# A fused encoder block: one projection as seven block products, its weight sums made during attention

## The chip, the cores and the metric

The kernel runs on one core of a Trainium2 chip. The metric is the device time of one execution in microseconds. The core's engines work side by side, each through its own list of instructions: TensorE (PE in the profile; PEld is its loading of weights), VectorE (DVE), ScalarE (ACT), GpSimd (POOL) and SyncE (SP), which here only issues DMAs. They wait for each other through semaphores.

## The reference

One layer of an encoder, in float32, for 512 + 256 tokens with 16 meta tokens; width 1024, MLP width 4096.

```python
u = _rms(h, norm_mix[l])
proj = u @ w_in[l]
...
attn = _mla_attention(q_n, q_r, k_n, k_r, v).reshape(B, L, N_HEADS * V_DIM) @ w_o_attn[l]
a, b = jnp.split(conv_in, 2, axis=-1)
c = a * jax.nn.sigmoid(b)
c = lax.conv_general_dilated(...) + conv_b[l]
c = jax.nn.silu(_layernorm(c, conv_ln_g[l], conv_ln_b[l]))
conv = c @ w_conv_out[l]
g_a, g_c = jnp.split(jax.nn.sigmoid(gate_logits + b_gate[l]), 2, axis=-1)
h = h + (g_a * attn + g_c * conv) @ w_out[l]
u = _rms(h, norm_mlp[l])
h = h + jnp.square(jax.nn.relu(u @ w_mlp_in[l])) @ w_mlp_out[l]
```

The final RMSNorm follows. The change concerns `c @ w_conv_out` and the sums of weight blocks that this product, `w_out` and `w_mlp_out` use.

## The kernel before, in words

**Products.** Every float32 product is three matmuls of rounded parts: of each operand a *high* is made (a copy in the rounded type, on ScalarE) and a *low* (the operand minus its high, on GpSimd or VectorE), and high x high, high x low and low x high are added in PSUM. The 768 tokens are the columns, as 512 + 256, or as two halves of 384 (THIRD).

**Seven block products.** The output projection (units U_OUT), the first MLP product (U_IN) and the second (U_FF) are done as seven products of 2 x 2 blocks in place of eight: each product takes one block or a signed sum of blocks of either side. Sums of weight blocks are needed for them: `isums`, `osums` and `wsums` in DRAM, each made by a DMA copy of one block (issued by SP) and an accumulating DMA of the next one (issued by GpSimd, `accum_op=ALU.add`); those of the MLP are made during the stages before, those of the second MLP in attention, four sums, two halves per pair of heads (lines 730 and 1907). Three-block sums and negated blocks of the MLP are made in the ring itself: ScalarE negates a landed block (line 1159) and GpSimd adds the second block to it by DMA (line 2015).

**The stages around the change.** Attention runs over four pairs of heads. Then comes the attention branch's projection (U_O, 8 units of 128 output rows), its result gated into `zacc` by VectorE (line 1581); beside it the convolution branch's LayerNorm is finished: squares on ScalarE (1089), their sum on GpSimd, the variance by a matmul with ones after unit 4, root (1097), reciprocal (1604), scaling (1591), silu (1102), highs (1105) and lows (1596) of c. Then the convolution branch's projection (U_CO, 8 units, matmuls of line 543): per unit m VectorE multiplies the result in PSUM with the gate (`gconv`, 1646) and adds it to `zacc` (1651). Between these it makes the sums (`zsum`, 1622) and lows (`zlo`, 1629) of zacc's blocks that the output projection reads, and ScalarE their highs (1120). The output projection (matmuls of line 2343) and the MLP (2373 and 2394) follow.

**Order.** There is no scheduler: each engine's list is written out by hand, and an engine runs it in that order. The weights come through a ring of raw slots loaded by SP, each load waiting until a slot's last user is done; high slots are fewer than raw ones, so ScalarE's highs follow TensorE's units closely.

## Time and profile before

| | us |
|---|---|
| median of 3 runs (lowest, highest) | 1244.06 (1241.23, 1245.78) |
| the profiled execution | 1243.28 |
| its span in the trace | 1241.7 |
| TensorE busy | 1211.0 |
| VectorE busy | 895.5 |
| ScalarE busy | 553.6 |
| GpSimd busy | 431.2 |

The profile is of one execution. Busy time is the time in which an engine worked at instructions; span is first to last instruction. The chain of waits goes back from the last instruction to what released each step. The mean granted clock of TensorE is 0.999 of 2.4 GHz. Attention fills the stretch to 577 us, the attention branch's projection that to 637, the convolution branch's that to 705, the output projection that to some 763, and the two MLP products the rest.

### The profile page before, as it was taken

To read this page: it belongs to the slowest core of one execution; us is meant where nothing else is said; L and a number is where in the kernel's file an instruction comes from. 1 tells how busy PE (TensorE), PEld (TensorE's weight loads), DVE (VectorE), ACT (ScalarE), POOL (GpSimd) and SP (SyncE) were. 2 spreads that over 40 slices of the span, in tenths; PEclk is the share of its full clock that TensorE was granted. 3 is DMA by queue.
4 is the path that set the end of the run, shared out by engine and by line. 5 is a ranking of instruction groups with operands and counts; after the bars stand their busy time and mean duration, and the time that the engine had idled before them with its cause. 6 is when DMAs were issued, how large, how long until landed. Compare 5 with 4: busy or idle time off the path is not lost.

```text
span 1241.7 us, 18362 instructions
## 1 busy us (share of the span) xinstructions
PE 1211.0 (98%) x6797; PEld 1075.9 (87%) x6797; DVE 895.5 (72%) x1043; ACT 553.6 (45%) x814; POOL 431.2 (35%) x299
## 2 busy tenths in 40 slices
PE   6999999999999999999999999999999999999997
PEld 5888888888888889987888888999989988887886
DVE  4115999999986666677374766586769796677887
ACT  6234211222245666664352346545553244445555
POOL 2454434488855555464744263000120000002101
PEclk9999999999999999999999999999999999999999
DMA  6347888899899796957798343334793343348633
GB/s 194 94 136 158 201 200 177 203 232 236 190 252 230 168 226 177 274 109 182 201 215 247 107 135 119 109 130 122 181 204 120 120 152 127 128 134 207 176 129 118
DMA packets 174370, 211.70 MB, mean 170 GB/s; under 512 B 13040, under 2 KB 125742, under 8 KB 174301
## 3 DMA queue, kind: packets, MB, share of 16 engines
q1 hardware_dynamic: 136300, 155.19, 40.3%
q0 software_dynamic: 35696, 49.29, 24.3%
q10 hardware_dynamic: 2304, 6.29, 1.3%
q8 instruction: 45, 0.74, 0.2%
q14 instruction: 25, 0.20, 0.0%
HBM read 201.31 MB, written 88.08 MB: 233 GB/s over the span
## 4 chain that ended last, share of the span: by engine, by line
PE 79%; issue 6%; DMA 5%; POOL 3%; DVE 3%; ACT 3%; SPq 1%; POOLq 0%; ACTq 0%; DVEq 0%
PE psum L543 34%; PE psum L2394 17%; PE psum L2373 14%; PE psum L2343 5%; DMA raw<-in_w_mlp_in 2%; PE psum L2196 2%; PE psum L2226 1%; POOL wlo L530 1%; PE psum L2069 1%; DMA rawx<-in_w_mlp_in 1%; DMA wsums<-in_w_mlp_out 1%; PE psum L2208 1%; DMA rawx<-in_w_mlp_out 1%; POOL isums L1902 0%; DVE olo L1536 0%
## 5 line engine op out<-in xcount | busy, mean ns | idle before, releaser
L530 POOL TENSOR_TENSOR wlo<-raw,whi 128x1024 fp32r<-128x1024 f32 (+1 forms) x72 | 167.9, 2332 | 200.0 <-ACT whi L525 199.8
L1377 DVE SCALAR_TENSOR_TENSOR psum<-cs,convw,psum 128x799 f32<-128x799 f32 x196 | 189.4, 1049 | 0.0
L543 PE MATMUL psum<-uhi,whi 128*128 128x512 f32 x592 | 152.4, 338 | 0.8 <-POOL wlo L530 0.8
L543 PE MATMUL psum<-uhi,wlo 128*128 128x512 f32 x592 | 152.9, 339 | 0.0
L543 PE MATMUL psum<-ulo,whi 128*128 128x512 f32 x592 | 152.5, 339 | 0.0
L525 ACT ACTIVATE whi<-raw 128x1024 fp32r<-128x1024 f32 (+1 forms) x73 | 72.1, 987 | 108.3 <-PE psum L543 97.5
L543 PEld LDWEIGHTS psum<-uhi,whi 128*128 128x128 f32 x592 | 91.4, 188 | 14.8 <-POOL wlo L530 1.6
L543 PEld LDWEIGHTS psum<-uhi,wlo 128*128 128x128 f32 x592 | 91.6, 188 | 12.9
L2373 PE MATMUL psum<-u2hi,whi 128*128 128x384 f32 x296 | 100.0, 338 | 2.5 <-DVE rawlo L1772 1.4
L543 PEld LDWEIGHTS psum<-ulo,whi 128*128 128x128 f32 x592 | 91.5, 188 | 12.5
L2373 PE MATMUL psum<-u2hi,rawlo 128*128 128x384 f32 x304 | 101.7, 334 | 0.0
L2373 PE MATMUL psum<-u2lo,whi 128*128 128x384 f32 x296 | 99.0, 334 | 0.0
L1168 ACT ACTIVATE whi<-raw 128x1024 fp32r<-128x1024 f32 x55 | 58.1, 1058 | 76.7 <-PE psum L2394 40.7
L2394 PE MATMUL psum<-whi,hidhi 128*128 128x512 f32 x222 | 86.4, 389 | 0.0
L2394 PE MATMUL psum<-whi,hidlo 128*128 128x512 f32 x222 | 86.4, 389 | 0.0
L2394 PE MATMUL psum<-rawlo,hidhi 128*128 128x512 f32 x216 | 84.0, 389 | 0.0
L2015 POOL DMA_DIRECT2D raw<-in_w_mlp_out x6 | 7.2, 1195 | 214.0 <-ACT raw L1159 214.0
L1758 DVE TENSOR_TENSOR hid<-hid,psum 128x768 f32<-128x768 f32 x64 | 59.5, 951 | 30.0 <-ACT hid L1241 19.2
L2373 PEld LDWEIGHTS psum<-u2hi,whi 128*128 128x128 f32 x296 | 55.6, 188 | 3.4 <-DVE rawlo L1772 1.9
L2373 PEld LDWEIGHTS psum<-u2hi,rawlo 128*128 128x128 f32 x304 | 57.1, 188 | 0.0
L935 ACT ACTIVATE gout<-psum,vec 128x768 f32<-128x768 f32 x16 | 14.4, 902 | 93.9 <-PE psum L543 93.9
L2373 PEld LDWEIGHTS psum<-u2lo,whi 128*128 128x128 f32 x296 | 55.6, 188 | 0.0
(294 smaller groups left out, 3099.2 us busy)
## 6 DMA issues: line engine op xcount, KB each, us to landing
raw<-in_w_in SPq DMA_DIRECT2D x38, 512.0 KB, 4.4
isums<-in_w_mlp_in SPq DMA_DIRECT2D x32, 512.0 KB, 7.8
isums<-in_w_mlp_in POOLq DMA_DIRECT2D x32, 512.0 KB, 8.1
wsums<-in_w_mlp_out SPq DMA_DIRECT2D x32, 512.0 KB, 10.5
wsums<-in_w_mlp_out POOLq DMA_DIRECT2D x32, 512.0 KB, 10.1
raw<-isums SPq DMA_DIRECT2D x24, 512.0 KB, 3.3
raw<-wsums SPq DMA_DIRECT2D x20, 512.0 KB, 3.2
raw<-in_w_mlp_out SPq DMA_DIRECT2D x16, 512.0 KB, 3.8
```

Source lines behind the costliest of these rows:

```text
L525: nc.scalar.activation(whi[:, c % 2, 0:w], raw[:, c % 4, 0:w], ACT.Copy).then_inc(hi_ready, 1)
L530: gp.tensor_tensor(out=wlo[:, c % 2, 0:w], in0=raw[:, c % 4, 0:w], in1=whi[:, c % 2, 0:w].bitcast(F32), op=ALU.subtract).then_inc(lo_ready, 1)
L543: mm = nc.tensor.matmul(out[:, o0:o0 + n], a, b[:, k, c0:c0 + n], start=first and step == 0, stop=last and step == 2)
L935: nc.scalar.activation(gout[:, c % 2], psum[:, c % 2, 0:TQ], ACT.Sigmoid, bias=vcol("b_gate", i * 4 + c)).then_inc(gate_ready, 1)
L1168: nc.scalar.activation(mhi[high(U_IN + x)], mraw[place(U_IN + x)], ACT.Copy).then_inc(mhi_ready, 1)
L1377: ins = nc.vector.scalar_tensor_tensor(out=out, in0=src, scalar=w, in1=a, op0=ALU.mult, op1=ALU.add)
L1758: nc.vector.tensor_tensor(out=block_, in0=block_, in1=c_banks(m), op=ALU.add if sign > 0 else ALU.subtract).then_inc(hid_added, 1)
L2069: mm = nc.tensor.matmul(bank[:, 2 * n + seg, 0:w], a[:, k], b[:, k, c0:c0 + w], start=k == 0 and step == 0, stop=k == KD - 1 and step == 2)
L2196: mm = nc.tensor.matmul(psum[:, q % 2, e * HALF:e * HALF + n], a[:, c0:c0 + P], b[:, grp["k0"] + k0:grp["k0"] + k0 + n], start=step == 0, ...
L2343: mm = nc.tensor.matmul(bank[:, OUT_MIX[p]["banks"][tt]], a, b[:, kk, :], start=OUT_MIX[p]["new"] and jj == 0 and kk == 0 and step == 0, s ...
L2373: mm = nc.tensor.matmul(bank[:, 2 * in_pair(m) + e, 0:THIRD], a[:, k, e * P:(e + 1) * P], b, start=k == 0 and step == 0, stop=k == KD // 2 ...
L2394: mm = nc.tensor.matmul(bank[:, FF_BANKS[p % 2][tt]], a, b[:, kk, :], start=jj == 0 and kk == 0 and step == 0, stop=jj == STEPS - 1 and kk ...
```

## The change

The convolution branch's projection becomes seven block products as well, each in two halves J of the output rows: 14 units of 4 k x 2 x 3 matmuls with 384 columns (`CO_MIX`). Its four sums of weight blocks (`csums`, of three, two, two and four blocks, the longer ones built on the shorter ones) are made during attention by SP's copies (line 807) and GpSimd's accumulating DMAs (2117), in the place of the fourth sum of the second MLP. That sum is now made in the ring, by an accumulating DMA on the landed block (`x_added`, 2231). The sums of c's blocks are made by VectorE (`c_mix`, 1782 and 1785), 14 highs by ScalarE (1233) and 14 lows by VectorE (1793). A result that two products share is held: ScalarE copies a pair of banks to `xheld` or `zheld` (`co_hold`, 1250), and VectorE's drain (`co_drain`) adds it to another pair (1813), multiplies by a gate block (1816) and adds it to, or takes it from, zacc (1819). The sum of squares moves from GpSimd to VectorE, and the variance's matmul from after unit 4 to after unit 3 of the attention branch. Nearly all weight lows of both projections are GpSimd's now (VectorE keeps those of the convolution branch's units 1 and 2, and loses three of the output projection's), SP's and GpSimd's loops over the pairs are unrolled, and the output projection's seven additions of weight sums become four.

```diff
+CO_UNITS = 2 * 7
-SUMS = (((0, 1), (1, 1)), ((0, 0), (1, 0)), ((1, 0), (1, 1)), ((0, 0), (0, 1)))
+SUMS = (((0, 1), (1, 1)), ((0, 0), (1, 0)), ((1, 0), (1, 1)))
...
+CO_MIX = (
+    dict(a=((0, 0),), b=(0, 0), banks="X", new=True),
+    dict(a=((0, 1),), b=(1, 0), banks="Y", new=True),
+    dict(a=((1, 0), (1, 1), (0, 0)), banks="X", new=False),
+    dict(a=((1, 0), (1, 1)), banks="Z", new=True),
+    dict(a=((0, 0), (1, 0)), banks="X", new=False),
+    dict(a=((1, 0), (1, 1), (0, 0), (0, 1)), b=(1, 1), banks="Z", new=False),
+    dict(a=((1, 1),), banks="X", new=False),
+)
+CO_BLOCKS = ((0, 0, 1), (1, 1, 4), (0, 1, 5), (1, 0, 6))
+C_MIXED = tuple((p, part) for p in (T1, T2, T4, T3) for part in range(2))
+VECTOR_UNITS = (U_CO + 1, U_CO + 2)
...
+            def co_sum_copy(n):
+                sp.wait_ge(copy_landed[3], (STEPS + n) * 16)
+                if n // 2 in (1, 2):
+                    sp.wait_ge(sums_landed[3], (STEPS + n // 2 * 2) * 16)
+                sp.dma_start(co_sum(n), co_term(n, 0)).then_inc(copy_landed[3], 16)
...
-                    for c in range(4):
+                    for c in range(3):
                         sum_copy(c, i * 2 + h)
+                    co_sum_copy(i * 2 + h)
...
+            def gate_block(n):
+                half, tokens, _ = CO_BLOCKS[n % 4]
+                first = KD + 4 * half + n // 4 * 2
+                sp.wait_ge(merged, KD + n - 1)
+                sp.dma_start(gblock[:, n % 2], gates[first:first + 2, :, tokens * THIRD:(tokens + 1) * THIRD]
...
+            def co_hold(J, p, held):
+                act.wait_ge(unit_used, U_CO + 7 * J + p + 1)
+                if p == 0:
+                    wait(act, gated, 7 * J - 2)
+                if p == 2:
+                    act.wait_ge(gated, 7 * J + 1)
+                if p == 3:
+                    wait(act, gated, 7 * J - 4)
+                nc.scalar.activation(held[:, :, :], pair_banks(co_pair(J, p)), ACT.Copy).then_inc(co_held, 1)
...
+            for p, part in C_HIGHS[4:8]:
+                c_high(p, part)
+            co_hi(0)
+            for p, part in C_HIGHS[8:10]:
+                c_high(p, part)
+            co_hi(1), co_hi(2)
+            for p, part in C_HIGHS[10:]:
+                c_high(p, part)
...
+            for v in range(CO_UNITS):
+                J, p = v // 7, v % 7
+                if p in (0, 2):
+                    co_hold(J, p, xheld)
+                if p == 3:
+                    co_hold(J, p, zheld)
+                if v + 3 < CO_UNITS:
+                    co_hi(v + 3)
+                else:
+                    out_hi(v + 3 - CO_UNITS)
...
+            def co_drain(J, e):
+                half, tokens, p = CO_BLOCKS[e]
+                n, done = 4 * J + e, 7 * J + 2 * e
+                held = (xheld, zheld, xheld, None)[e]
...
+                dve.wait_ge(merged, KD + n)
+                dve.wait_ge(unit_used, U_CO + 7 * J + p + 1)
+                if held is not None:
+                    dve.wait_ge(co_held, 3 * J + (1, 3, 2)[e])
+                    nc.vector.tensor_tensor(out=gconv[:, :, :], in0=pair_banks(co_pair(J, p)), in1=held[:, :, :], op=ALU.add).then_inc(gated, 1)
+                    dve.wait_ge(gated, done + 1)
+                dve.wait_ge(gin_landed[n % 2], 16 * (KD // 2 + n // 2 + 1))
...
+            c_mix(T4, 0), c_mix(T4, 1)
+            gate_attn(6)
+            c_low(T1, 0), c_low(T1, 1)
+            gate_attn(7)
+            ring_lo(U_CO + 1)
+            c_low(T2, 0), c_low(T2, 1)
+            ring_lo(U_CO + 2)
+            c_low(T4, 0), c_low(T4, 1)
+            c_mix(T3, 0), c_mix(T3, 1)
+            for p in (T3, 5):
+                c_low(p, 0), c_low(p, 1)
...
+                if p == 2:
+                    pe.wait_ge(co_held, 3 * J + 1)
...
+                if p == 6:
+                    pe.wait_ge(gated, 7 * J + 3)
...
+                if u == 0:
+                    pe.wait_ge(gated, 12)
...
+            def x_add(x):
+                if x_added(x):
+                    if x_negated(x):
+                        gp.wait_ge(wneg_ready, negated_before(x + 1))
                     else:
+                        gp.wait_ge(m_landed[place(U_IN + x)], landed(U_IN + x))
+                        gp.wait_ge(mhi_ready, x - 2)
                     gp.dma_start(x_place(x), x_block(x, 1), accum_op=ALU.add).then_inc(wsum_landed[x % 3], 16)
```

How the rows of an engine's list stand, before and after, at three places. ScalarE where the convolution branch's projection starts, before: silu (L1102), highs of c, weight highs (L525), and the first high of z.

```order
L1102 ACTIVATE cs<-cs,vec 128x768 [waits ln_scaled]
L1105 ACTIVATE chi<-cs 128x768 [waits c_silu]
L525 ACTIVATE whi<-raw 128x1024 [waits unit_used,raw_landed1]
L1102 ACTIVATE cs<-cs,vec 128x768 [waits ln_scaled]
L1105 ACTIVATE chi<-cs 128x768 [waits c_silu]
L525 ACTIVATE whi<-raw 128x1024 [waits unit_used,raw_landed2]
L525 ACTIVATE whi<-raw 128x1024 [waits unit_used,raw_landed3]
L1120 ACTIVATE zhi_118<-zacc 128x768 [waits merged]
L525 ACTIVATE whi<-raw 128x1024 [waits unit_used,raw_landed0]
```

And after: highs of c and of its sums (L1233), weight highs (L1239), the held copies (L1250).

```order
L1239 ACTIVATE whi<-raw 128x1024 [waits unit_used,raw_landed0]
L1233 ACTIVATE chi_125<-csum_139 128x768 [waits mixed] x2
L1239 ACTIVATE whi<-raw 128x1024 [waits unit_used,raw_landed1]
L1239 ACTIVATE whx<-raw 128x1024 [waits unit_used,raw_landed2]
L1233 ACTIVATE chi_123<-csum_137 128x768 [waits mixed] x2
L1233 ACTIVATE chi_124<-cs 128x768 [waits unit_used,c_silu] x2
L1250 ACTIVATE xheld<-psum 128x768 [waits unit_used]
L1239 ACTIVATE whi<-raw 128x1024 [waits unit_used,raw_landed3]
L1239 ACTIVATE whi<-rawx 128x1024 [waits unit_used,m_landed4]
L1250 ACTIVATE xheld<-psum 128x768 [waits gated,unit_used]
L1239 ACTIVATE whx<-rawx 128x1024 [waits unit_used,m_landed5]
```

Four highs of c's blocks, two of them of sums that VectorE makes last, stand directly ahead of the first held copy; before, nothing but weight highs stood there.

VectorE in the convolution branch's projection, before: product with the gate, addition, and between them lows and sums of zacc's blocks.

```order
L1629 TENSOR_TENSOR zlo_124<-zacc,zhi_118 128x768 [waits z_hi]
L1622 TENSOR_TENSOR zsum_135<-zacc 128x768 [waits merged]
L1646 TENSOR_TENSOR gconv<-psum,gin 128x768 [waits merged,gin_landed1,unit_used]
L1651 TENSOR_TENSOR zacc<-zacc,gconv 128x768 [waits merged,gated]
L1646 TENSOR_TENSOR gconv<-psum,gin 128x768 [waits merged,gin_landed0,unit_used]
L1651 TENSOR_TENSOR zacc<-zacc,gconv 128x768 [waits merged,gated]
L1629 TENSOR_TENSOR zlo_124<-zacc,zhi_118 128x768 [waits z_hi]
L1629 TENSOR_TENSOR zlo_129<-zsum_135,zhi_123 128x768 [waits z_hi]
L1622 TENSOR_TENSOR zsum_135<-zacc 128x768 [waits merged]
L1646 TENSOR_TENSOR gconv<-psum,gin 128x768 [waits merged,gin_landed1,unit_used]
L1651 TENSOR_TENSOR zacc<-zacc,gconv 128x768 [waits merged,gated]
```

After, between the drains of the second half's first two blocks (drains 4 and 5):

```order
L1813 TENSOR_TENSOR gconv<-psum,xheld 128x768 [waits co_held,unit_used,merged]
L1816 TENSOR_TENSOR gconv<-gconv,gblock 128x768 [waits gin_landed0,gated]
L1819 TENSOR_TENSOR zacc<-zacc,gconv 128x2x384 [waits gated]
L1865 TENSOR_TENSOR zsum_155<-zsum_154,zacc 128x768 [waits mixed,unit_used,merged]
L1865 TENSOR_TENSOR zsum_157<-zacc 128x768 [waits unit_used,merged]
L1872 TENSOR_TENSOR zlo_148<-zsum_154,zhi_142 128x768 [waits mixed,z_hi]
L1872 TENSOR_TENSOR zlo_146<-zacc,zhi_140 128x768 [waits z_hi]
L1865 TENSOR_TENSOR zsum_156<-zsum_155,zacc 128x768 [waits mixed,unit_used,merged]
L1872 TENSOR_TENSOR zlo_149<-zsum_155,zhi_143 128x768 [waits mixed,z_hi]
L1872 TENSOR_TENSOR zlo_151<-zsum_157,zhi_145 128x768 [waits z_hi]
L1813 TENSOR_TENSOR gconv<-psum,zheld 128x768 [waits co_held,unit_used,merged]
L1816 TENSOR_TENSOR gconv<-gconv,gblock 128x768 [waits gin_landed1,gated]
```

Where one or three instructions stood between two of VectorE's drains, seven now stand between these two, and each drain has three instructions in the place of two.

SP at the end of a pair's loads, before: eight copies for the sums, each waiting only for the copy before it of the same sum.

```order
L730 ISA [waits copy_landed1]
L730 DMA wsums<-in_w_mlp_out 256x1x512
L730 ISA [waits copy_landed2]
L730 DMA wsums<-in_w_mlp_out 256x1x512
L730 ISA [waits copy_landed3]
L730 DMA wsums<-in_w_mlp_out 256x1x512
L730 ISA [waits copy_landed0]
L730 DMA wsums<-in_w_mlp_out 256x1x512
```

After, in the second pair of heads (the loads of the next pair begin at the last row):

```order
L824 DMA wsums<-in_w_mlp_out 256x1x512 [waits copy_landed2]
L807 DMA csums<-csums 128x1024 [waits sums_landed3,copy_landed3]
L824 DMA wsums<-in_w_mlp_out 256x1x512 [waits copy_landed0]
L824 DMA wsums<-in_w_mlp_out 256x1x512 [waits copy_landed1]
L824 DMA wsums<-in_w_mlp_out 256x1x512 [waits copy_landed2]
L807 DMA csums<-csums 128x1024 [waits sums_landed3,copy_landed3]
L846 DMA raw<-in_w_uq 128x4x64 [waits lo_ready]
```

A copy for csums takes the fourth place and waits also for GpSimd's additions to have landed.

## Rows read from the trace of the kernel before

**Rows 1.** The page: TensorE's busy time, and the chain that ended last.
```profile
PE 1211.0 (98%) x6797; PEld 1075.9 (87%) x6797; DVE 895.5 (72%) x1043; ACT 553.6 (45%) x814; POOL 431.2 (35%) x299
...
PE 79%; issue 6%; DMA 5%; POOL 3%; DVE 3%; ACT 3%; SPq 1%; POOLq 0%; ACTq 0%; DVEq 0%
```

**Rows 2.** Windows: start:end, us, each engine's busy us, clock, DMA share, GB/s.
```profile
577.00:637.00 60.00, 60.00 (x334) 51.28 (x334) 36.95 (x29) 27.81 (x31) 37.41 (x20) 1.00 0.90 224
637.00:705.00 68.00, 68.00 (x386) 59.00 (x385) 36.02 (x30) 17.62 (x20) 25.64 (x10) 1.00 0.69 193
```

**Rows 3.** The chain of waits, 577 to 780 us: start, us, what.
```profile
578.34 31.80 PE psum L543 x180
...
611.43 93.28 PE psum L543 x528
704.72 48.97 PE psum L2343 x216
...
771.90 5.23 PE psum L2373 x30
```

**Rows 4.** VectorE in time: start, us, line, names, [idle before <- releaser].
```profile
613.54 4.95 DVE L1604 RECIPROCAL lnr<-lnacc 128x768 f32<-128x768 f32 x1 [2.40 <-ACT lnacc L1097]
...
633.65 1.01 DVE L1591 SCALAR_TENSOR_TENSOR cs<-cs,vec,lnr 128x768 f32<-128x768 f32 x1
...
639.39 0.95 DVE L1581 TENSOR_TENSOR zacc<-psum,gin 128x768 f32<-128x768 f32 x1
...
653.87 0.96 DVE L1646 TENSOR_TENSOR gconv<-psum,gin 128x768 f32<-128x768 f32 x1 [6.53 <-PE psum L543]
```

**Rows 5.** ScalarE in time, in the convolution branch's stage.
```profile
637.64 0.85 ACT L1105 ACTIVATE chi<-cs 128x768 fp32r<-128x768 f32 x1
...
653.93 1.06 ACT L525 ACTIVATE whi<-raw 128x1024 fp32r<-128x1024 f32 x1 [7.42 <-PE psum L543]
```

**Rows 6.** VectorE and GpSimd in time, 629 and 663 us.
```profile
629.48 0.95 DVE L1581 TENSOR_TENSOR zacc<-psum,gin 128x768 f32<-128x768 f32 x1
...
629.63 2.41 POOL L530 TENSOR_TENSOR wlo<-raw,whi 128x1024 fp32r<-128x1024 f32 x1 [4.41 <-ACT whi L525]
...
663.55 3.00 POOL L530 TENSOR_TENSOR wlo<-raw,whi 128x1024 fp32r<-128x1024 f32 x1 [5.47 <-ACT whi L525]
...
664.22 3.15 DVE L1629 TENSOR_TENSOR zlo<-zacc,zhi 128x768 fp32r<-128x768 f32 x1
```

**Rows 7.** The gates' loads, line 780.
```profile
DMA to landing us min/median/max: 2.9/4.7/13.8
```

**Rows 8.** GpSimd's additions in the ring, line 2015, 1100 to 1160 us.
```profile
L2015 POOL DMA_DIRECT2D raw<-in_w_mlp_out x6: 1188/1197/1202, 1119.7 to 1152.4; - x6
...
DMA to landing us min/median/max: 7.2/8.3/9.7
```

**Rows 9.** Waits of TensorE, 1004 to 1242 us: total, times, longest.
```profile
PE psum L2394 <- DVE hidlo L1793: 1.1, 1, 1.1
```

**Rows 10.** The page: DMA issues, KB each, median us to landing.
```profile
wsums<-in_w_mlp_out SPq DMA_DIRECT2D x32, 512.0 KB, 10.5
wsums<-in_w_mlp_out POOLq DMA_DIRECT2D x32, 512.0 KB, 10.1
...
raw<-in_w_mlp_out SPq DMA_DIRECT2D x16, 512.0 KB, 3.8
```

**Rows 11.** SP, GpSimd and ScalarE in time, in attention's second pair.
```profile
393.16 0.39 SPq L752 DMA_DIRECT2D raw<-in_w_uq  x1
...
406.44 1.52 POOL L1907 DMA_DIRECT2D wsums<-in_w_mlp_out  x1
...
436.06 0.63 ACT L525 ACTIVATE whi<-raw 128x512 fp32r<-128x512 f32 x1
```

**Rows 12.** The loads of the next pair's weights, line 752.
```profile
DMA to landing us min/median/max: 2.2/3.9/19.3
```

**Rows 13.** A window of attention, columns as in rows 2.
```profile
416.00:426.00 10.00, 10.00 (x77) 9.59 (x76) 6.81 (x10) 7.38 (x12) 5.09 (x4) 1.00 0.20 53
```

More of the change, by code:

```diff
@@ L234, in x_negated, with x_added @@
     return (IN_MIX[IN_ORDER[x][0]] if x < IN_UNITS else MIX[x // STEPS - len(IN_MIX)]).get("negate", False)
+def x_added(x):
+    return x_negated(x) or (x >= IN_UNITS and len(MIX[x // STEPS - len(IN_MIX)]["b"]) > 1 and
+                            MIX[x // STEPS - len(IN_MIX)]["b"] not in SUMS)
 def negated_before(x):
@@ L242, in summed_before @@
 def summed_before(x, slot):
-    return sum(x_negated(y) for y in range(slot, x, 3))
+    return sum(x_added(y) for y in range(slot, x, 3))
 def posted(p):
@@ new lines, in c_low, with ring_lo @@
+            def c_low(p, part):
+                dve.wait_ge(c_hi, C_HIGHS.index((p, part)) + 1)
+                if p in (T1, T2):
+                    dve.wait_ge(mixed, C_MIXED.index((T2 if p == T1 else T4, part)) + 1)
+                nc.vector.tensor_tensor(out=clo[p][:, 2 * part:2 * part + 2, :], in0=c_source(p, part),
+                                        in1=chi[p][:, 2 * part:2 * part + 2, :].bitcast(F32), op=ALU.subtract).then_inc(c_lo, 1)
+            def ring_lo(n):
+                dve.wait_ge(hi_ready, n + 1)
+                nc.vector.tensor_tensor(out=mlo[place(n)], in0=mraw[place(n)], in1=mhi[high(n)].bitcast(F32),
+                                        op=ALU.subtract).then_inc(inlo_ready, 1)
@@ new lines, in co_drain @@
+            def co_drain(J, e):
+                half, tokens, p = CO_BLOCKS[e]
+                n, done = 4 * J + e, 7 * J + 2 * e
+                held = (xheld, zheld, xheld, None)[e]
+                gate = gblock[:, n % 2]
+                made = zacc[:, 4 * half + 2 * J:4 * half + 2 * J + 2, tokens * THIRD:(tokens + 1) * THIRD]
+                dve.wait_ge(merged, KD + n)
[5 more added lines that the diff above has]
+                dve.wait_ge(gin_landed[n % 2], 16 * (KD // 2 + n // 2 + 1))
+                nc.vector.tensor_tensor(out=gconv[:, :, :], in0=gconv[:, :, :] if held is not None else pair_banks(co_pair(J, p)), in1=gate,
+                                        op=ALU.mult).then_inc(gated, 1)
+                dve.wait_ge(gated, done + (2 if held is not None else 1))
+                nc.vector.tensor_tensor(out=made, in0=made, in1=gconv[:, :, :],
+                                        op=ALU.add if half == 0 else ALU.subtract).then_inc(merged, 1)
@@ L1602, in _ @@
+            gate_attn(0)
+            for j in range(KD):
+                centre(range(j, j + 1))
+                if j > 1:
+                    ln_sq_add(j - 1)
+                if j == 3:
+                    gate_attn(1)
+            ln_sq_add(KD - 1)
+            gate_attn(2), gate_attn(3)
             dve.wait_ge(ln_root, 1)
@@ L2005, in _ @@
-            for u in range(OUT_UNITS):
-                if u not in OUT_VECTOR:
-                    gp.wait_ge(hi_ready, U_OUT + u + 1)
-                    gp.tensor_tensor(out=mlo[place(U_OUT + u)], in0=mraw[place(U_OUT + u)], in1=mhi[high(U_OUT + u)].bitcast(F32),
-                                     op=ALU.subtract).then_inc(lo_ready, 1)
-            def x_add(x):
-                if x_negated(x):
-                    gp.wait_ge(wneg_ready, negated_before(x + 1))
+            out_sum_add(2)
@@ new lines, in _ @@
+            lo_unit(gp, U_O, 0, 4)
+            lo_unit(gp, U_O, 1, 1)
+            out_sum_add(1)
+            lo_unit(gp, U_O, 1, 2)
+            lo_unit(gp, U_O, 1, 3)
+            for n in range(U_CO, U_IN):
+                if n not in VECTOR_UNITS:
+                    gp.wait_ge(hi_ready, n + 1)
+                    gp.tensor_tensor(out=mlo[place(n)], in0=mraw[place(n)], in1=mhi[high(n)].bitcast(F32),
+                                     op=ALU.subtract).then_inc(lo_ready, 1)
+                if n == U_CO:
+                    out_sum_add(3)
@@ L2335, in _ @@
                         h_transposes(n)
-                wh, wl = (w.rearrange("p (k n) -> p k n", k=2) for w in (mhi[high(U_OUT + u)], mlo[place(U_OUT + u)]))
                 for kk in range(2):
```

398 lines of the change are left out of this document (235 added, 163 removed).

## The prediction

> **What bounds the kernel now.** I read the page first, then the table of windows, then the chain of waits, and last the rows in time of each engine around the stages that change. The page says that TensorE is busy 98% of the span and holds 79% of the chain that ended last [rows 1]: time is lost or won where its matmuls become fewer or where it has to wait. The windows show no gap on it from 577 to 705 us, the two branch projections [rows 2]. The chain gives the size of the units there: 93.28 us for 528 matmuls is 11 units of 48, 8.48 us each; the last eight are the convolution branch's, from 636.9 to 704.7 us [rows 3]. VectorE and GpSimd have room in this stage: VectorE works 36 of 68 us and often sits 6.5 us before a unit's gate product, GpSimd works 26 us [rows 2, 4]. This room is what the change spends.
>
> **Matmuls, the gain.** Removed are 8 x 48 matmuls of the convolution branch, 8 x 8.48 = 67.8 us. Added are 14 units of 4 x 2 x 3 = 24 matmuls over 384 columns. The MLP's matmuls of that width take 5.23 us per 30, 0.1743 us each [rows 3], so a unit takes 4.18 us and 336 matmuls 58.6 us: **-9.3 us**. Clock and kind of operand are the same. A rule would make it less: by the Trainium skill, TensorE: Matmul & The Clock Gate, Back-to-back issue gap, a lone matmul costs its columns at 2.4 GHz plus a small fixed term of 2.5 ns. By it a pair of 512 and 256 columns is 325 ns and one of 384 is 162.5 ns, an estimate of 62.4 - 54.6 = 7.8 us won. The rows give 353 ns for the pair and 174 ns for the one, so the measured widths decide.
>
> **The first products and their held banks.** What is new stands ahead of the projection: eight sums of column blocks of c and 14 lows on VectorE, in the place of 8 lows; 14 highs on ScalarE, in the place of 8. In return the variance's matmul goes one unit (8.48 us) earlier, since its sum no longer needs GpSimd; the reciprocal, 4.95 us from 613.54 [rows 4], can start near 605.5 and is over before the gate of unit 4, which ends near 612.4. From there to the end of the last sum (T3) VectorE has 8 scalings, 8 sums, 3 gates and 10 lows, 29 of 0.95 us (six from 633.65 to 639.39 in rows 4), and 2 weight lows of 1024 elements, 1.25 us by their size: 30.0 us, to 642.4. But a VectorE operation with both inputs in SBUF and GpSimd's weight low run one after the other: 0.95 us became 3.15 beside one of GpSimd's, and GpSimd's 2.41 became 3.00 [rows 6]; gates, whose input is PSUM, ran beside one undisturbed [rows 6]. Three weight lows of GpSimd fall in this stretch; with two of them in the way, 2.1 us each, the T3 sums end near 646.6. ScalarE takes its instructions in order, and ahead of the first held copy stand the highs of T3 and of block 5, so three highs of 0.85 us [rows 5] follow the last sum (649.1) and then the copy itself (649.9). Unit 2 needs that copy and its turn is 636.9 + 2 x 4.18 = 645.3: a **wait of 4.6 us**, a new one. Bounds: 0.4 if VectorE never waits for GpSimd, 6.7 with one collision more. I take two, since the one shown and three like it in this stage of before each cost VectorE 2.1 or 2.2 us.
>
> **Drains and the start of the output projection.** In the 58.6 us of the new units VectorE gets 37 operations (22 of the eight drains, 7 sums of z, 8 lows) and GpSimd 12 weight lows. Eight of the 37 read PSUM; the other 29, at 0.95 us, and 12 x 2.41 us on GpSimd [rows 6] exclude each other: 27.6 + 28.9 = 56.5 of 58.6 us. The gaps that VectorE had are gone, and a chain of drains runs behind TensorE. One place in full: unit 13 (its turn 636.9 + 4.6 + 13 x 4.18 = 695.8) waits for the first addition of drain 5. Drain 4 follows the end of unit 8 (679.1) with three operations; then stand seven operations with both inputs in SBUF, and the addition: 679.1 + 11 x 0.95 = 689.6. ScalarE makes the high of S3, for the last of them, only after the held copy that waits for unit 10 (687.5) and a weight high, so the addition ends no earlier than 691. Four weight lows of GpSimd fall in between; three in the way, 2.2 us each, make it 697.7: 1.9 us. In the same way the output projection's unit 0 waits 1.1 us for the last drain's product, unit 2 1.3 us for the sum behind it, and one later unit 1.2 us for its weight low, since all of these lows are GpSimd's now (three were VectorE's) and ScalarE's highs for them stand behind z's highs. Sum **5.5 us**. Bounds: 0 (the operations find the gaps) and 10 (each of the four costs one collision more); gate blocks are loaded behind each drain as before, and gates of the same 0.39 MB landed after 4.7 us in the median but up to 13.8 [rows 7]; at 9 us each drain would start some 4 later.
>
> **One sum of the second MLP in the ring.** The last product of it, 8 units, gets its weight sum by accumulating DMAs from GpSimd in the ring, not from memory. The eight that exist (six of them in the row shown) were issued from 1119.7 to 1152.4, every 4.67 us, against 4.08 us for a unit (18 matmuls of 48.97 / 216 us) [rows 3, 8]; they landed after 8.3 us, and TensorE waited once, 1.1 us [rows 8, 9]. The new ones have no negation ahead of them, and a unit is loaded five units (20.4 us) ahead; load, add, high and low take 3.8 + 8.3 + 1.06 + 1.25 = 14.4 of it [rows 5, 8, 10], and up to six more where the add stands behind the high of the unit two ahead of it. I take **+0.5**; the bounds are 0 and 8 x (4.67 - 4.08) = 4.7.
>
> **Attention.** Eight copies and eight accumulating DMAs of 512 KB go, eight and eight of the same size come. Unrolling the loops of SP and GpSimd changes no order. I take 0 here; the new wait that it hides is a rival. The output projection's weight sums become cheaper (7 additions to 4, on a queue that nobody waited for): 0.
>
> **Sum.** -9.3 + 4.6 + 5.5 + 0.5 = +1.3 us on the profiled execution, whose span of 1241.7 us and 1.6 around it make 1243.3: 1244.6. The median of the runs shown, 1244.06, is 0.8 above that execution, so by it 1245.4; I predict **1245 us**, no difference. What a measurement of this kernel can tell from no change is about 0.5%, 6.2 us.
>
> **Rivals.**
> 1. *Faster: VectorE and GpSimd find their gaps.* If collisions are rarer than I count, the first wait shrinks to 0.4 and the later ones to some 3, the bare order of the drains behind the units: -9.3 + 0.4 + 3 + 0.5 = -5.4, 1238.7 by the median, and with none at all 1234.8. For it: the 6.5 us gaps before each gate product now [rows 4]. Against: every weight low of GpSimd that met an operation of VectorE with two inputs in SBUF cost it time [rows 6]. 0.26; in 0.20 of it the waits are fewer still, and it ends under 1237.8.
> 2. *Slower: SP stands in attention.* SP's copies for the new sums wait for an add of GpSimd to land, and behind them on SP stand the next pair's weight loads. Before, those went out at 393.16 for a high at 436.06 [rows 11]. The add that the copy needs goes out at 406.44 [rows 11] and lands after 10.1 us in the median; the copy then must land before the next one is issued, after 10.5 in the median [rows 10]: the loads go out at 417 + 9 = 426. With the median landing of 3.9 us they are in time; with 13 (the longest was 19.3) [rows 12] they are 3 us late, and so again one pair later. From a landing of 10 us on it decides. Price: 2 x 2.6 = 5.2 us (I take 0.4 of the 3 as slack behind the high), to 1250.6 by the median. For it: landings of over 10 us are common in attention [rows 10]. Against: from 416 to 426 us the DMA share is 0.20 [rows 13], so nothing else stands in their way then. 0.15.
> 3. *Slower by the drains:* gate blocks that land after 9 us, or one more collision at each wait: some 4.3 more, 1249.7. 0.08.
> 4. *The ring cannot keep pace at the end:* +4.7 instead of 0.5, 1249.6. 0.05.
> 5. *It doesn't do what it says:* the matmul count would be as before. The code issues 336 in place of 384; 0.01.
>
> **How the numbers follow.** My forecast (waits that add up to 7 to 13 us in place of 9.3) has 0.45 and its own range is 1241 to 1249. Rivals 1 and 2 put the ends. The range that holds 8 in 10 is **1236 to 1251.5**: below it 0.08, the case with nearly no waits; above it 0.12, rival 2 with a part of 3 or 4. Faster by over 0.5% (below 1237.8): 0.20. Slower by over 0.5% (above 1250.3): 0.20, rival 2 on top of the sum, 3 and 4 with a part of it. Within: 0.60.
>
> **What would show it.** The span of the new units in the chain of waits: 4.18 us a unit and 336 matmuls show the gain. A wait of TensorE's 384-column matmuls for ScalarE's xheld at 645 to 650 us shows the first term; if that wait is absent, the collisions are over-counted. Waits for gconv, zacc and a weight low between 690 and 720 us show the second. Operations of VectorE with 3.15 us beside GpSimd's lows show the mechanism of both. Waits for rawlo or whi of the second MLP's last units show the fourth term; an idle TensorE at 436 to 440 and 487 to 490 us, with SP's copies of csums ahead of the loads, shows rival 2. I am wrong if the fourteen units end more than 4 us away from 636.9 + 58.6 + 4.6 + 1.9 = 702.0, or if attention ends more than 2 us away from where it did.

## The result, and the profile after

| | before | changed |
|---|---|---|
| median of 20 runs, us | 1242.85 | 1247.22 |
| profiled execution, us | 1243.28 | 1249.21 |
| its span, us | 1241.7 | 1247.6 |

The ratio is 1.0031 (95% interval 1.0018 to 1.0043), which is 3.9 us slower; the two medians of the table lie 4.4 us apart. That is inside the band that the prediction called no difference, on the slow side of it, and the interval excludes 1. The changed kernel's trace is of an execution 2.0 us above its median.

First the page of the changed kernel, against [rows 1]:

```profile
PE 1207.2 (97%) x6749; PEld 1078.7 (86%) x6749; DVE 930.3 (75%) x1069; ACT 568.0 (46%) x832; POOL 439.1 (35%) x303
...
PE 79%; DVE 6%; issue 6%; DMA 4%; ACT 2%; POOL 2%; POOLq 0%; SPq 0%; DVEq 0%; ACTq 0%
```

TensorE is busy 3.8 us less and the span is 5.9 us longer; VectorE's share of the chain doubled. Where that is, the windows tell (columns as in rows 2):

```profile
577.00:637.00 60.00, 59.50 (x331) 50.65 (x330) 48.10 (x42) 31.09 (x35) 23.46 (x11) 1.00 0.78 211
637.00:705.00 68.00, 61.85 (x342) 60.80 (x342) 58.59 (x43) 29.87 (x34) 35.59 (x15) 0.95 0.68 211
```

Against [rows 2], TensorE is idle for 6 of 68 us, VectorE works 58.6 us in place of 36.0, and the mean granted clock of the stage is 0.95. The chain of waits at its start (start, us, what) shows both:

```profile
640.64 8.33 PE psum L2555 x48
648.97 4.00 issue
652.97 7.12 PE psum L2555 x26
```

48 matmuls take 8.33 us, 4.17 a unit, as the 384-column row of [rows 3] said. Then comes the wait at unit 2, and the next 26 take 7.12 us where 4.5 would do. Who is waited for, in ScalarE's and VectorE's rows in time, and how TensorE's matmuls follow behind the wait:

```profile
649.00 1.71 ACT L1233 ACTIVATE chi<-csum 128x768 fp32r<-128x768 f32 x2 [6.25 <-DVE csum L1785]
650.62 1.56 ACT L1233 ACTIVATE chi<-cs 128x768 fp32r<-128x768 f32 x2
652.08 0.79 ACT L1250 ACTIVATE xheld<-psum 128x768 f32<-128x768 f32 x1
```

```profile
616.12 9.66 DVE L1760 SCALAR_TENSOR_TENSOR cs<-cs,vec,lnr 128x768 f32<-128x768 f32 x8
...
634.87 4.01 DVE L1782 SCALAR_TENSOR_TENSOR csum<-csum,cs 128x768 f32<-128x768 f32 x2
...
648.02 1.81 DVE L1785 TENSOR_TENSOR csum<-cs 128x768 f32<-128x768 f32 x2
```

```profile
652.97 0.66 PE L2555 MATMUL psum<-chi,whx 128*128 128x384 f32 x1 [4.00 <-issue]
653.43 0.52 PE L2555 MATMUL psum<-clo,whx 128*128 128x384 f32 x1
653.75 0.52 PE L2555 MATMUL psum<-chi,rawlo 128*128 128x384 f32 x1
```

The two rows of 9.66 and 4.01 us are where VectorE met GpSimd's lows (eight scalings and two sums, each row some 2.2 us over its own time). The sums of T3 end at 649.8; four highs stand before xheld, which ends at 652.9. The trace runs 3.8 to 3.9 us later than that of before from the first attention matmul (362.9 against 359.0) to the start of this stage, so in the time of before the wait is where it was forecast. Behind it 15 matmuls come about 0.32 us apart in place of 0.17. In windows:

```profile
649.00:653.00 4.00, 0.03 (x1) 0.06 (x1) 3.96 (x5) 3.97 (x6) 0.00 (x0) 0.79 1.10 349
653.00:660.00 7.00, 7.00 (x27) 7.00 (x28) 6.93 (x4) 1.98 (x3) 5.42 (x2) 0.63 0.06 18
```

The granted clock is 0.63 of 2.4 GHz in the 7 us after 4 us of an idle TensorE: part of them at 1.2 GHz, the rest at 2.4. Set against 0.17 us each, the slow matmuls lose 2.5 us.

The other waits of TensorE, from 637 to 770 us (total, times, longest):

```profile
PE psum L2555 <- issue: 6.2, 2, 4.0
PE psum L2590 <- DVE zacc L1819: 1.2, 1, 1.2
PE psum L2590 <- POOL wlo L2218: 0.8, 1, 0.8
PE psum L2590 <- issue: 0.7, 1, 0.7
```

The two of L2555 are units 2 and 13. These views count only the idle time between two records; measured start to start over the matmul's own time, the five waits lose 4.2, 2.3, 0.8, 1.4 and 1.0 us.

The second of them, at unit 13, is a wait for VectorE's first addition of drain 5 (`gconv`, L1813), and VectorE came to it late. Rows of GpSimd and VectorE in time, between drains 4 and 5:

```profile
690.75 3.07 POOL L2218 TENSOR_TENSOR rawlo<-raw,whi 128x1024 fp32r<-128x1024 f32 x1 [1.75 <-ACT whi L1239]
691.48 3.15 DVE L1872 TENSOR_TENSOR zlo<-zsum,zhi 128x768 fp32r<-128x768 f32 x1
...
694.91 2.86 POOL L2218 TENSOR_TENSOR rawlo<-raw,whi 128x1024 fp32r<-128x1024 f32 x1 [1.09 <-ACT whi L1239]
695.42 3.16 DVE L1865 TENSOR_TENSOR zsum<-zsum,zacc 128x768 f32<-128x768 f32 x1
...
702.45 0.94 DVE L1813 TENSOR_TENSOR gconv<-psum,zheld 128x768 f32<-128x768 f32 x1
702.58 2.37 POOL L2218 TENSOR_TENSOR rawlo<-raw,whi 128x1024 fp32r<-128x1024 f32 x1 [1.74 <-ACT whi L1286]
703.43 2.34 DVE L1816 TENSOR_TENSOR gconv<-gconv,gblock 128x768 f32<-128x768 f32 x1
```

All four weight lows that GpSimd makes between 685 and 701 us hold off an operation of VectorE with two inputs in SBUF, by 2.0 to 2.2 us each. The last weight low that unit 13 itself needs is the one from 694.91; it ended 5.7 us before the unit began, so it was not GpSimd that TensorE waited for.

The stages, each from its first matmul to the next stage's first (the last to the start of its last matmul), in every trace of the study. The first matmul of attention's projection stands among attention's last ones, at 563.6 us in the trace of before; this table begins the stage there.

| trace | attention | attention's projection | convolution's projection | output projection | first MLP | second MLP |
|---|---|---|---|---|---|---|
| before | 204.6 | 73.1 | 67.9 | 58.5 | 241.2 | 229.8 |
| e4, before with unrolled loops | 204.4 | 72.6 | 66.6 | 58.5 | 239.4 | 229.8 |
| changed | 204.5 | 73.1 | 68.1 | 61.3 | 238.8 | 231.3 |
| e10, changed again | 204.4 | 72.7 | 68.4 | 61.3 | 239.1 | 231.2 |
| e1 | 204.5 | 72.4 | 66.9 | 60.6 | 238.2 | 231.8 |
| e2 | 204.4 | 72.4 | 62.7 | 61.7 | 239.4 | 231.5 |
| e3 | 204.6 | 73.1 | 68.0 | 60.6 | 238.6 | 229.7 |
| e5 | 204.3 | 72.5 | 60.1 | 60.7 | 241.4 | 232.9 |
| e6 | 204.5 | 72.7 | 65.6 | 61.4 | 241.1 | 231.5 |
| e7 | 204.6 | 72.4 | 66.3 | 61.3 | 239.9 | 230.8 |
| e8 | 204.5 | 72.4 | 60.1 | 60.7 | 239.2 | 230.2 |
| e9 | 204.4 | 73.1 | 68.0 | 61.3 | 239.4 | 230.0 |

By stages the change costs 0.2 + 2.8 + 1.5 = 4.5 us in the two traces. What lies ahead of attention took 357.3 to 363.0 us over the twelve traces, and the first MLP 238.2 to 241.4. Neither goes with the kernel: e9 is the changed kernel up to the second MLP and has 357.3 where that has 362.9, and the two traces of the same matmuls in before and e4 have 241.2 and 239.4. In e5 and e6 some 1.6 us of the first MLP are again matmuls 0.32 us apart, about ten of them behind a wait of 1.8 us.

### The profile page after: what moved, and what is told of

It is laid out like the page before. It is cut to its first block, busy times and chain, and to the rows that moved or that the text cites. A ratio compares the mean times of both kernels' runs of the same rounds, so it can differ in the third digit from the quotient of the medians.

```text
span 1247.6 us, 18015 instructions
## 1 busy us (share of the span) xinstructions
PE 1207.2 (97%) x6749; PEld 1078.7 (86%) x6749; DVE 930.3 (75%) x1069; ACT 568.0 (46%) x832; POOL 439.1 (35%) x303
## 4 chain that ended last, share of the span: by engine, by line
PE 79%; DVE 6%; issue 6%; DMA 4%; ACT 2%; POOL 2%; POOLq 0%; SPq 0%; DVEq 0%; ACTq 0%
PE psum L584 30%; PE psum L2641 16%; PE psum L2620 15%; PE psum L2555 4%; PE psum L2590 4%; PE psum L2412 3%; PE psum L2442 2%; DMA rawx<-in_w_mlp_in 2%; PE psum L2285 2%; PE psum L2375 1%; DMA raw<-in_w_mlp_in 1%; PE psum L2424 1%; DVE hmix L2003 1%; PE psum L2259 1%; DVE ptlo L1640 1%
## 5 line engine op out<-in xcount | busy, mean ns | idle before, releaser
L571 POOL TENSOR_TENSOR wlo<-raw,whi 128x1024 fp32r<-128x1024 f32 (+1 forms) x64 | 144.7, 2261 | 182.7 <-ACT whi L566 182.5
L2231 POOL DMA_DIRECT2D raw<-in_w_mlp_out x12 | 14.4, 1196 | 258.4 <-ACT raw L1329 209.9
L566 ACT ACTIVATE whi<-raw 128x1024 fp32r<-128x1024 f32 (+1 forms) x64 | 62.5, 977 | 75.7 <-PE psum L584 65.2
L2620 PE MATMUL psum<-u2hi,rawlo 128*128 128x384 f32 x288 | 96.3, 334 | 0.0
L2641 PE MATMUL psum<-whi,hidhi 128*128 128x512 f32 x228 | 89.0, 390 | 1.7 <-DVE hidlo L2014 1.7
L2641 PE MATMUL psum<-rawlo,hidhi 128*128 128x512 f32 x228 | 88.7, 389 | 0.0
L2231 POOL DMA_DIRECT2D raw<-in_w_mlp_in x5 | 6.4, 1288 | 135.8 <-ACT raw L1329 135.8
```

The source lines that it names most:

```text
L566: nc.scalar.activation(whi[:, c % 2, 0:w], raw[:, c % 4, 0:w], ACT.Copy).then_inc(hi_ready, 1)
L571: gp.tensor_tensor(out=wlo[:, c % 2, 0:w], in0=raw[:, c % 4, 0:w], in1=whi[:, c % 2, 0:w].bitcast(F32), op=ALU.subtract).then_inc(lo_ready, 1)
L2620: mm = nc.tensor.matmul(bank[:, 2 * in_pair(m) + e, 0:THIRD], a[:, k, e * P:(e + 1) * P], b, start=k == 0 and step == 0, stop=k == KD // 2 ...
L2641: mm = nc.tensor.matmul(bank[:, FF_BANKS[p % 2][tt]], a, b[:, kk, :], start=jj == 0 and kk == 0 and step == 0, stop=jj == STEPS - 1 and kk ...
```

## The experiments

Each ratio is to the kernel before, timed beside it on the same chip.

**e1.** The first held copy ahead of the last highs.

```diff
             co_hi(1), co_hi(2)
+            co_hold(0, 0, xheld)
+            co_hi(3)
             for p, part in C_HIGHS[10:]:
                 c_high(p, part)
...
-                if p in (0, 2):
+                if p in (0, 2) and v > 0:
                     co_hold(J, p, xheld)
...
-                if v + 3 < CO_UNITS:
+                if v == 0:
+                    pass
+                elif v + 3 < CO_UNITS:
                     co_hi(v + 3)
```

> The first held copy (xheld) and the weight high of unit 3 stand on ScalarE ahead of the highs of T3 and block 5; nothing else is changed. Theory A (ScalarE's order alone makes the 4.0 us wait at unit 2): the wait and the 2.5 us of matmuls at half clock behind it go, and nothing else moves: 6 to 6.5 us less than the changed kernel, 1240.8. Theory B (the order only decides where the wait stands; VectorE and GpSimd, which exclude each other, are the bound of the stage): the wait of unit 2 goes, waits of 1 to 1.4 us appear at units 4 and 5 and the one at unit 13 grows from 2.3 to about 4, the sum of waits stays near 9 to 10 us, and only the clock's 2.5 us are won: 1244.7. If one of the new waits is long enough to lower the clock, even less. I hold B, 0.65.

Measured: 1.0007 (0.9992 to 1.0022). Waits of TensorE, 636 to 775 us:

```profile
PE psum L2559 <- issue: 5.0, 2, 2.8
PE psum L2594 <- POOL wlo L2222: 0.8, 1, 0.8
PE psum L2594 <- DVE zacc L1823: 0.7, 1, 0.7
```

and the windows around the longest:

```profile
655.00:658.60 3.60, 0.79 (x5) 0.50 (x4) 3.53 (x5) 1.06 (x2) 0.00 (x0) 1.00 0.01 3
658.60:662.60 4.00, 4.00 (x15) 4.00 (x16) 3.07 (x2) 3.19 (x4) 2.95 (x2) 0.57 0.48 154
```

The wait at unit 2 is gone and one of 2.8 us stands at unit 4, with a low clock behind it (0.57 over 4 us). Unit 13 waits 2.3 us start to start as in the changed kernel, but here this wait too has a low clock behind it (0.57 from 699.8 to 703.8 us, 1.00 in the changed kernel). The convolution branch's projection has 66.9 us for 68.1: theory A is false. B is right in that the wait moves. It is wrong in where it puts it, in the sum of the waits, which fell from 9.7 to 7.1 us, and in that the clock would be won back: the slow matmuls lose 3.3 us at two places, 2.5 at one in the changed kernel. By the ratios this is 3 us less than the changed kernel, with intervals that overlap; the trace has 1.9 us in the two projections.

**e2.** Weight lows of the convolution branch's units on VectorE. Same order as e1, and eleven `ring_lo` more between VectorE's sums, lows and drains, of which one is shown:

```diff
-VECTOR_UNITS = (U_CO + 1, U_CO + 2)
+VECTOR_UNITS = (U_CO + 1, U_CO + 2, U_CO + 3, U_CO + 4, U_CO + 5, U_CO + 6, U_CO + 7, U_CO + 8, U_CO + 9, U_CO + 10, U_CO + 11, U_CO + 12, U_CO + 13)
...
             co_drain(0, 0)
+            ring_lo(U_CO + 5)
...
```

> As the one before, and VectorE makes the weight lows of all convolution-branch units but the first (11 more, 1.23 us each), GpSimd none of them (it would take 2.41 us each). Theory B (exclusion): time in which either engine holds the other off falls by 11 x 1.2 = 13 us, no operation of VectorE lasts 3.1 us in the stage, the waits in the stage fall from 9.7 us to about 3, and the clock stays up: about 9 us less than the changed kernel, 1238, some 4 to 5 us under the kernel before. Rival (VectorE is full by its own work, 36 us + 13.5 us in 58.6): the lows on VectorE delay the drains, and the time stays at 1245 or above. I hold the first, 0.7.

Measured: 0.9996 (0.9981 to 1.0011). The stage took 62.7 us; this is the first theory, by half of its amount (4.4 us less than the changed kernel, 9 expected). Waits of TensorE in the two projections, 6.4 us start to start where about 3 were expected, and the rows in front of the longest:

```profile
PE psum L2589 <- DVE rawlo L1803: 2.4, 1, 2.4
PE psum L2624 <- DVE zacc L1823: 1.8, 1, 1.8
PE psum L2624 <- POOL wlo L2252: 0.8, 1, 0.8
PE psum L2589 <- issue: 0.8, 1, 0.8
```

```profile
671.53 0.96 DVE L1820 TENSOR_TENSOR gconv<-psum,gblock 128x768 f32<-128x768 f32 x1 [3.73 <-DMA gblock<-gates]
...
673.40 1.22 DVE L1803 TENSOR_TENSOR rawlo<-raw,whx 128x1024 fp32r<-128x1024 f32 x1
```

Until 693 us no VectorE operation of the stage lasts longer than 1.22 us, and VectorE has time to sit idle for a gate block. This block was issued at 662.5, behind 3 MB of h on the same queue, and landed 9 us later; unit 8's low stood behind the drain that needed the block. The remaining 2.4 us of wait did not lower the clock (1.00 in the 4 us behind it).

**e3.** The last product's weight sum in memory again.

```diff
-SUMS = (((0, 1), (1, 1)), ((0, 0), (1, 0)), ((1, 0), (1, 1)))
+SUMS = (((0, 1), (1, 1)), ((0, 0), (1, 0)), ((1, 0), (1, 1)), ((0, 0), (0, 1)))
...
-            whole = csums[CO_SUMS.index(a)] if len(a) > 1 else co_part(a[0])
+            whole = co_part(a[0])
...
-                    for c in range(3):
+                    for c in range(4):
                         sum_copy(c, i * 2 + h)
-                    co_sum_copy(i * 2 + h)
...
```

The kernel leaves out the four sums of the convolution branch's weights, their copies and their additions.

> The last product of the second MLP takes its weight sum from memory again, made in attention as in the kernel before; the four sums for the convolution branch are left out (its units load a plain block in their place, so the result of that product is another). The price of the sum in the ring: as forecast +0.5 us, from the traces of the two kernels up to 1.5 (stage of the second MLP 229.8 us before, 231.3 after), so this kernel is 0.5 to 1.5 us faster than the changed one, and the waits for hidlo at the end of the second MLP are those of before (one, 1.1 us). Rival (the sum in the ring costs more than the two traces show, since its additions compete with the loads): 3 us or more.

Measured: 1.0006 (0.9995 to 1.0017). The second MLP took 229.7 us against 231.3, to a tenth what it was before, with one wait of 1.1 us. So in the traces the sum in the ring costs 1.5 us, the upper end of what was expected. The ratio is 3.1 us below the changed kernel's, more than the 1.5; the stages account for 2.4 of it, 0.7 in the output projection, whose first wait is absent here. Two ratios with intervals of some 1.5 us to either side do not tell 1.5 from 3.1 us, so it is the stage alone that speaks against the rival.

**e4.** The kernel before with `peel=PAIRS` for SP's and GpSimd's loops.

> The kernel before with SP's and GpSimd's loops over the four pairs of heads unrolled, nothing else. As forecast: no difference to the kernel before, within 0.1%. Rival (longer instruction lists of SP and GpSimd delay the start: the changed kernel's trace begins its first projection 3.9 us later than the trace of before): 2 to 4 us slower, and the first projection starts at 44 to 45 us in place of 41.

Measured: 0.9992 (0.9978 to 1.0005), and the shortest lead to attention but one (357.9 us). Unrolling costs nothing that this can show, and the late start of the changed kernel's trace is not its doing.

**e5.** e2 with three orders changed.

```diff
             for v in range(3, CO_UNITS):
                 co_load(v)
...
                 if v == 8:
                     gate_block(2)
-                    sp.wait_ge(c_lo, len(C_LOWS))
...
                 if 10 <= v <= 12:
                     gate_block(v - 7)
+                if v == 12:
+                    sp.wait_ge(c_lo, len(C_LOWS))
...
             co_drain(1, 2)
+            co_drain(1, 3)
             z_low(1, 0)
             z_mix(S1, 1), z_mix(S2, 1), z_mix(S3, 1)
-            co_drain(1, 3)
...
             z_high(S1, 1)
+            out_hi(3)
             z_high(S2, 1), z_high(S3, 1)
```

(The loads of h move with the wait for c_lo that stands ahead of them.)

> The lows of the convolution branch's units on VectorE as in e2, and three orders changed by what e2's trace shows: SP loads h (3 MB) behind gate block 5 and not ahead of gate block 3 (which landed after 9 us and held a drain and unit 8's low, 2.5 us); VectorE makes the last drain before the next sums of z (1.9 us of wait at the output projection's unit 2); ScalarE makes the weight high of its unit 3 two instructions earlier (1.0 us). Theory B: nearly all waits of TensorE in the two projections are gone (about 1 to 1.5 us left of 6.4), so 5 us less than e2: 1237 to 1238, a ratio to the kernel before of 0.995 to 0.9965. Rival: each wait closed opens the next one behind it, and it stays at e2's ratio of 0.9996.

Measured: 0.9964 (0.995 to 0.9978), 1237.09 us against 1241.86, the time that was expected. The trace is of the slowest of the nine executions (1242.88 us). Waits of TensorE in both projections:

```profile
PE psum L2627 <- DVE h L1940: 1.0, 1, 1.0
PE psum L2592 <- issue: 0.8, 1, 0.8
PE psum L2627 <- DVE zlo L1893: 0.7, 1, 0.7
```

Four waits of 6.4 us became three of 2.9 us start to start (1 to 1.5 were expected), and two of them stand at new places: a low of z and an addition to h. The convolution branch's projection takes 60.1 us; its matmuls alone are 58.6.

**e6.** e5's orders, `VECTOR_UNITS` as in the changed kernel.

> The same orders as e5, but GpSimd makes the weight lows again (VectorE keeps units 1 and 2). If the orders alone did it, this is as fast as e5. If the exclusion of VectorE and GpSimd is what binds (theory B), it stays near e1: waits of 8 to 9 us in all, the longest (3 to 4 us) at unit 13, where drain 5 comes late, with half-clock matmuls behind it, and a ratio to the kernel before of 1.000 to 1.002. I hold the second, 0.75.

Measured: 1.0001 (0.9989 to 1.0013).

```profile
PE psum L2581 <- issue: 4.5, 2, 2.3
PE psum L2616 <- DVE zlo L1890: 1.2, 1, 1.2
PE psum L2616 <- DVE h L1929: 1.0, 1, 1.0
PE psum L2616 <- issue: 0.7, 1, 0.7
```

8.2 us of waits start to start, at units 4 and 13 and at three places of the output projection. Orders alone leave them; with the lows moved 2.9 are left. Between e5 and e6 only the engine of the lows and their places in its list differ, and this is worth 5.5 us in the first projection and 0.7 in the next, 1.6 of it slow matmuls behind unit 4; by the ratios, whose intervals are apart, it is 4.6 us. (Both traces are of the slowest execution of their kernel.) In e5 GpSimd makes no low between 636 and 691 us and VectorE's longest operation there takes 1.22 us; in e6 eight of VectorE's take 2.1 to 3.2 us beside one of GpSimd's lows. The wait at unit 13 was 2.3 and not 3 to 4 us, and the low clock stood behind the one at unit 4 (0.57 over 4 us) and not behind it.

**e7.** The wait filled with matmuls.

```diff
+                if v == 2:
+                    for n in range(21):
+                        nc.tensor.matmul(bank[:, n % 2, 0:THIRD], wh[:, n % 4, 0:P], chi[0][:, n % 4, :], start=True, stop=True)
                 if p == 2:
                     pe.wait_ge(co_held, 3 * J + 1)
```

> The changed kernel with 21 matmuls more (384 columns, into two banks that nothing reads before they are overwritten) where TensorE waits 4.0 us for the first held copy: 21 x 0.174 = 3.7 us, so they fit into the wait. If the 0.32 us matmuls behind that wait come from the clock alone, which fell to half in it, they are 0.17 us again: unit 2 starts at the same time and the stage is 2.5 us shorter than in the changed kernel (ratio to the kernel before 1.001 in place of 1.0031). Rival (something else slows them, such as the 276 to 349 GB/s of DMA traffic in that stretch, or VectorE and ScalarE at the same banks): they stay at 0.32 us, and nothing is won.

Measured: 1.003 (1.0014 to 1.0046). Its windows:

```profile
645.00:649.00 4.00, 3.17 (x19) 2.85 (x18) 3.95 (x5) 3.98 (x6) 0.00 (x0) 1.00 1.06 342
649.00:653.00 4.00, 4.00 (x25) 4.00 (x23) 3.93 (x4) 1.55 (x2) 3.32 (x2) 1.00 0.04 12
```

The DMA traffic and the other engines are as they were (342 GB/s against 349), and the 25 matmuls behind take 4.0 us: what slowed them was the clock. The stage has 66.3 us for 68.1. It would be 2.3 us less, but TensorE came to it 0.5 us earlier against VectorE's sums than in the changed kernel's trace; the two branch projections together fall by 2.5 us, as expected. The ratio does not show it: its interval just misses the 1.001 that was expected, and it just includes the 1.0017 that the stage's 1.8 us would leave of the changed kernel's 1.0031.

**e8.** e5, and three multiplications of GpSimd earlier. **e9.** The changed kernel with that alone.

```diff
             for m in range(FF_UNITS):
+                if m == 6 * STEPS:
+                    for i in range(TT):
+                        y_gains(i)
                 x_add(IN_UNITS + m)
-                if Y_SCALE <= m < Y_SCALE + TT:
-                    y_gains(m - Y_SCALE)
```

The reason, from VectorE and GpSimd in time in the changed kernel:

```profile
1200.46 3.02 DVE L2003 TENSOR_TENSOR hmix<-hid 128x768 f32<-128x768 f32 x1
```

```profile
1200.15 1.19 POOL L2231 DMA_DIRECT2D raw<-in_w_mlp_out  x1 [4.01 <-DMA raw<-in_w_mlp_out]
1200.88 1.78 POOL L2243 TENSOR_TENSOR h<-h,gfinal 128x512 f32<-128x512 f32 x1
```

> e5, and GpSimd makes its first three multiplications by the final gain ahead of the eight additions of the last product's weight sums, where the kernel before has them in time (1172 to 1182 us); in the changed kernel they stand behind additions that wait for the ring and fall at 1201 to 1212 us, on VectorE's hmix, which then takes 3.0, 2.0 and 2.9 us in place of 0.95. Theory: the second MLP's stage falls by what these collisions cost TensorE, from 231.3 to 232.9 us to about 230.5, 1 to 2 us: a ratio to the kernel before of about 0.995. Rival (the additions land too late, the collisions cost nothing): the same as e5, 0.9964, with the waits for hidlo near the end still there.

> The changed kernel with only that move of three multiplications. If the price of the sum in the ring is these collisions, the second MLP's stage takes 229.8 to 230.5 us in place of 231.3, and the ratio to the kernel before falls from 1.0031 to about 1.002; if the additions themselves are late, it stays at 231.3.

Measured: e8 0.9939 (0.9919 to 0.9958), 1235.77 us against 1242.68, the fastest kernel of the study; e9 1.0017 (1.0004 to 1.003). The second MLP takes 230.2 and 230.0 us, in place of 232.9 (e5) and 231.3 (changed), and hmix 0.95 us again. The last product's eight units show it alone: against the kernel before they take 1.4 us more in the changed kernel (1.2 in its second trace), 2.3 in e5, and nothing more in e8 and e9, where the additions are still made. So what the sum in the ring costs in its own units is these collisions, all of it, and not the additions; what is left of the differences, 0.1 to 0.9 us, stands earlier in the stage, around its first waits for hidlo, which the kernel before has too. That the medians of e8 (six runs) and e5 (nine) differ is not shown by their intervals, nor that e9 is faster than the changed kernel; the stages show it.

**e10.** The changed kernel again.

> The changed kernel once more, for a second trace of it and a comparison on the same chip: ratio 1.002 to 1.004. Open is whether the half-clock matmuls behind the 4.0 us wait belong to every execution. e7 removed them in its trace and its median did not fall (1.0030), which speaks for executions in which the clock holds: then unit 2's matmuls may come every 0.17 us here, at the same wait of 4.0 us. If they come every 0.32 us again, e7's median stays unexplained.

Measured: 1.0025 (1.0009 to 1.004). Again 4.0 us of wait, again matmuls 0.32 us apart, the same five waits to 0.05 us. In e3 and e9, which have the same wait, the matmuls behind it are slow too (10 of them in e3, 15 in e9), so it belongs to all four traces of this wait. The mean granted clock, which is on record for every execution, says the same: on average 0.9948 for the changed kernel (20 executions, none above 0.997), 0.9944 in e10 and 0.9963 in e7. Over 1245 us that makes, as an estimate, 13, 14 and 9 us at half the clock. So the fill kept the clock in e7's other executions too, and some 2 us should be won. Why the ratio of e7 does not show them stays open; its executions scatter from 1242.1 to 1251.4 us.

## Why the prediction was right, and where it was not

The result lies in the range, 2.2 us above the forecast of 1245, and 2.6 us above it in what the change costs (+3.9 by the ratio, +1.3 forecast). The main mechanism held: the gain of the matmuls, a first wait for the held copy and late drains behind collisions of VectorE and GpSimd. One cost, the clock, was missing, and the ring's was put down to the wrong thing. Part of the agreement is luck, as the terms show.

- **Matmuls, -9.3.** Measured 4.17 us a unit, 58.4 in all. The units of before take 8.48 us in its trace and 8.33 in e4's, so the gain is 8.2 to 9.4.
- **The first held copy, 4.6.** Measured 4.2 start to start (4.0 of idle time). T3's sums ended at 646.0 in the time of before (646.6 said), with two collisions of 2.2 us, as counted. Not counted was a wait of VectorE for ScalarE's silu (1.2 us at 629.6); the rest of its operations, 28.1 us in place of 30.0, made up for it. That the order on ScalarE was only the last link is shown by e1.
- **Drains and start of the output projection, 5.5.** Measured 2.3 + 0.8 + 1.4 + 1.0 = 5.5, against 1.9, 1.1, 1.3 and 1.2. For unit 13 the working said 18.6 us from the end of unit 8 to the addition, and 18.6 it was (684.8 to 703.4), by luck: four collisions in place of three, and 0.1 us of waiting for ScalarE in place of 1.4. Unit 0 of the output projection waits for drain 6's addition (ended 708.51), not for the last drain's product. That VectorE's operations were late by GpSimd's lows is in their rows; that the lows' engine is what binds, and not the orders, is shown by e5 against e6.
- **Missing: the clock.** The first wait was priced at its length. It cost 2.5 us more, since the 15 matmuls behind it ran at half clock (e7 fills the wait, and they do not). No row of before could show it: between its start and its end TensorE never sat idle for more than 1.5 us. This is the largest error of the sum.
- **The ring, 0.5.** Measured 1.5. The working looked at ring and landing times, and not at what else stood behind the new, waiting instructions on GpSimd: three multiplications that slid by 25 us onto VectorE's sums. This step failed as a mechanism; the price was inside its bounds.
- **Attention, 0.** Measured 204.5 against 204.6. Rival 2's order of events did come: SP's copies of csums stand ahead of the loads, which went out at 427.5 us, 423.6 in the time of before (426 said, 393.2 before the change). Its price did not: the loads of line 846 landed after 6.0 us in the median and 7.6 at most, and from 10 on it would have cost time. (Its working takes 9 us for a copy's landing where it names 10.5.)
- **Rivals 3 and 4.** A gate block held VectorE once, for 0.3 us (before 678.0); the ring cost 1.5 and not 4.7.
- **Sum.** -9.3 + 4.2 + 5.5 + 2.5 + 1.5 = +4.4 from these terms, 4.5 by the stages, 3.9 by the ratio; +1.3 was forecast. Clock and ring are the difference, less 0.4 of the first wait.

Rival 1, that collisions would be rarer, was false for this kernel and true for e5: the gap on VectorE that it pointed to exists, once GpSimd's lows are out of the way.

## What to carry to other kernels

Two engines whose operations exclude each other are one resource for these operations: add up their time together, and give the work to the one that does it in less of that time (1.22 us against 2.41 here), even if it is the busier one. Moving the operation that is waited for last shifts the wait (e1); taking work off the shared resource takes most of it away (8.2 to 2.9 us, e6 to e5). A wait of TensorE can cost more than its length, since the clock may fall behind it. When a waiting instruction is put on an engine, look far down its list for who will now run late and beside whom.
